# Expert weights in order of use, a new block order, a lighter end of the loop, and first modulation slices on TensorE

## The reference, cut to what matters

```python
c_act = jax.nn.silu(c)                       # one vector of 1024
mod = c_act @ w_ada[l] + b_ada[l]            # 1024 x 6144
sh1, sc1, g1, sh2, sc2, g2 = jnp.split(mod, N_ADA, axis=-1)
u = modulate(rmsnorm(h, norm_mix_g[l]), sh1, sc1)
...
# mixture of experts: 64 experts, each token goes to 8
def expert_block(args):
    toks, ws, e = args
    xb = u_pad[toks]
    hid = jax.nn.silu(xb @ we_gate[e]) * (xb @ we_up[e])
    return (hid @ we_down[e]) * ws[:, None]
```

## Time and profile before

| | |
|---|---|
| median of 3 runs | 3078.28 us (3076.34 to 3078.71) |
| profiled execution | 3077.83 us, span 3076.5 us |
| TensorE matmuls busy | 2711.3 us, 88% |
| VectorE, ScalarE, GpSimd busy | 1058.0, 706.2, 164.7 us |
| DMA | 423.89 MB, mean 138 GB/s over the span |

### The profile page before, as it was taken

How to read it: one execution, slowest core, us unless ns; L and a number is a source line. 1 busy time by engine, 2 the same in 40 slices (tenths; PEclk the granted TensorE clock), 3 DMA queues, 4 the chain that set the end, 5 groups by cost and what they waited for, 6 DMA issues and landing times.

```text
span 3076.5 us, 41132 instructions
## 1 busy us (share of the span) xinstructions
PE 2711.3 (88%) x16972; PEld 1598.5 (52%) x16972; DVE 1058.0 (34%) x2309; ACT 706.2 (23%) x1152; POOL 164.7 (5%) x126
## 2 busy tenths in 40 slices
PE   6999997999989898887989489979996988999797
PEld 2666664444437556564655234437875433555443
DVE  7665654322212212111211231026774113433312
ACT  2333331100011111111111110135552222333311
POOL 0000000000000112222222100000000000000000
PEclk8999998999998899898989789979997999999899
DMA  6222211333313998998898513221101211111110
GB/s 238 104 89 81 70 65 45 123 137 123 133 62 127 350 324 307 346 333 304 299 373 287 180 65 119 66 106 41 64 28 66 83 69 37 55 55 55 35 41 28
DMA packets 80746, 423.89 MB, mean 138 GB/s; under 512 B 16144, under 2 KB 16528, under 8 KB 37936
## 3 DMA queue, kind: packets, MB, share of 16 engines
q1 hardware_dynamic: 53296, 366.37, 30.9%
q0 software_dynamic: 17568, 35.71, 4.9%
q10 hardware_dynamic: 9696, 19.17, 1.7%
HBM read 392.79 MB, written 56.69 MB: 146 GB/s over the span
## 4 chain that ended last, share of the span: by engine, by line
PE 73%; DMA 11%; DVE 8%; ACT 5%; issue 3%; SPq 1%; POOLq 0%; POOL 0%; ACTq 0%; DVEq 0%
PE psum_all L277 33%; PE psum_all L1859 7%; PE psum_all L1419 7%; DMA total_rows<-big,rows 5%; PE psum_all L3253 4%; PE psum_all L2006 4%; PE psum_all L1466 3%; PE psum_all L3126 3%; PE psum_all L287 3%; DMA weights<-t_experts 2%; DMA big<-t_experts 2%; PE psum_all L302 1%; DMA big<-u_rows,rows 1%; PE psum_all L632 1%; DVE big L3387 1%
## 5 line engine op out<-in xcount | busy, mean ns | idle before, releaser
L277 PE MATMUL psum_all<-u,weights 128*128 128x512 f32 x1024 | 451.3, 598 | 12.2 <-issue 12.2
L277 PE MATMUL psum_all<-big,weights 128*128 128x512 f32 (+1 forms) x768 | 338.4, 596 | 6.7 <-DVE big L3419 4.2
L277 PEld LDWEIGHTS psum_all<-u,weights 128*128 128x128 f32 x1024 | 194.3, 192 | 248.0 <-issue 247.6
L1419 PE MATMUL psum_all<-weights,big 128*64 128x256 f32 (+2 forms) x1216 | 249.4, 407 | 49.0 <-DMA weights<-t_experts 35.1
L1419 PE MATMUL psum_all<-big 128*32 128x256 f32 (+2 forms) x1728 | 216.3, 404 | 35.6 <-DMA weights<-t_experts 19.0
L277 PEld LDWEIGHTS psum_all<-big,weights 128*128 128x128 f32 (+1 forms) x768 | 144.7, 189 | 194.6 <-issue 188.0
L1859 PE MATMUL psum_all<-big,weights 128*128 128x512 f32 x512 | 222.4, 597 | 14.0 <-DVE big L1929 14.0
L1419 PEld LDWEIGHTS psum_all<-weights,big 128*64 128x64 f32 (+2 forms) x1216 | 169.5, 160 | 88.3 <-issue 55.4
L1419 PEld LDWEIGHTS psum_all<-big 128*32 128x32 f32 (+2 forms) x1728 | 140.4, 135 | 74.7 <-issue 43.3
L1859 PEld LDWEIGHTS psum_all<-big,weights 128*128 128x128 f32 x512 | 98.1, 192 | 138.2 <-issue 134.8
L287 PE MATMUL psum_all<-const_cols,big 128*128 128x128 f32 (+2 forms) x892 | 129.5, 286 | 38.2 <-DMA big<-u_rows,rows 22.6
(11 more groups left out here) (343 smaller groups left out, 3399.2 us busy)
## 6 DMA issues: line engine op xcount, KB each, us to landing
big<-t_experts SPq DMA_DIRECT2D x96, 1024.0 KB
weights<-t_experts SPq DMA_DIRECT2D x96, 1024.0 KB
weights<-t_ada SPq DMA_DIRECT2D x24, 1024.0 KB, 6.9
weights<-t_rkvg SPq DMA_DIRECT2D x16, 1024.0 KB, 5.4
rwkv_inputs<-big ACTq DMA_DIRECT2D x48, 256.0 KB, 2.0
big<-rwkv_inputs SPq DMA_DIRECT2D x8, 1280.0 KB, 6.6
weights<-t_x SPq DMA_DIRECT2D x8, 1024.0 KB, 4.8
weights<-t_BC SPq DMA_DIRECT2D x8, 1024.0 KB, 4.8
```

The lines of the kernel that those rows point to most:

```text
L277: last = pe.matmul(out, lhsT, rhs, start=n == 0, stop=n == len(terms) - 1)
L1419: ins = pe.matmul(K.psum[rows, bank, n * F_E:(n + 1) * F_E], xT[:, k, rows], X.part(r, n, KD, F_E)[:, k, :], start=k == 0, stop=k == KD - 1)
```

## The change

Four edits:

1. The experts' parts are loaded in the order in which the products use them: for block b the gate parts, then the up parts, then the down parts of block b - 1. The register that holds the expert's number is read anew for each part, behind the wait.
2. `blocks()` yields the same blocks in another order.
3. Behind the loop for overflow blocks only VectorE drains, and only SyncE waits for it, before it loads `total_rows`.
4. For the first eight modulation slices, TensorE does the products: the column of c_act, repeated 32 times, is the stationary operand, the slice (256 columns) is the moving one. Row tile k goes to column group k mod 4, two tiles are accumulated in each group. VectorE copies the 128 x 256 result out, times 1/32, and TensorE sums over the partitions as before. The `pe_sum` products are spread between the slices. The table of constants comes in two loads: its first 256 columns (identity and ones) behind the first part of x, the rest behind all of x.

```diff
@@ start_act
-            act.dma_start(K.consts[:, :], A["shape_consts"][:, 0:CONST_SMALL]).then_inc(*K.consts_in.tick("all_in"))
+            act.dma_start(K.consts[:, 0:FIRST_CONSTS], A["shape_consts"][:, 0:FIRST_CONSTS]).then_inc(*K.ones_in.tick("all_in"))
+    act.dma_start(K.consts[:, FIRST_CONSTS:CONST_SMALL], A["shape_consts"][:, FIRST_CONSTS:CONST_SMALL]) \
+        .then_inc(*K.consts_in.tick("all_in"))
@@
+def pe_ada_rows(K, q, s, i):
+    pe, w, b = K.nc.tensor, K.W.tile(i, KD, 256), 4 + s % 2
+    K.bank(b, q.dve, "rows", s)
+    pe.wait_ge(*K.W.here(i))
+    for k in range(KD):
+        at = 32 * (k % 4)
+        ins = pe.matmul(K.psum[at:at + 32, b, 0:256], K.c_act[:, k:k + 1].to_broadcast([P, 32]), w[:, k, :],
+                        start=k < 4, stop=k >= 4)
+    ins.then_inc(*K.W.left(i, q.pe))
+
+def dve_ada_rows(K, q, s, i):
+    dve = K.nc.vector
+    if s >= 2:
+        dve.wait_ge(*q.pe.at("ada", s - 2))
+    dve.wait_ge(*q.pe.at("w", i))
+    dve.tensor_scalar(K.ada[s % 2][:, :], K.psum[:, 4 + s % 2, 0:256], 1.0 / 32, None, ALU.mult).then_inc(*q.dve.tick("rows", s))
+
+def pe_ada_sum(K, q, s):
+    pe, acc = K.nc.tensor, K.ada[s % 2]
+    pe.wait_ge(*q.dve.at("rows", s))
+    for half in range(2):
+        ins = pe.matmul(K.psum[:, 6, 2 * s + half:2 * s + half + 1], acc[:, half * P:half * P + P], K.c("ones")[:, 0:1],
+                        start=True, stop=True)
+    ins.then_inc(*q.pe.tick("ada", s))
@@ start_pe
+    pe.wait_ge(*q.act.at("c"))
+    for s in range(2):
+        pe_ada_rows(K, q, s, w0 + s)
+    pe.wait_ge(*K.ones_in.at("all_in"))
+    K.bank(6, q.dve, "mod")
+    for s in range(2, 8):
+        pe_ada_sum(K, q, s - 2)
+        if s in (2, 4, 5, 6):
+            k = max(0, 2 * s - 6)
+            pe_sum(K, q, "mix", k)
+            pe_sum(K, q, "mix", k + 1)
+        pe_ada_rows(K, q, s, w0 + s)
+    for s in (6, 7):
+        pe_ada_sum(K, q, s)
     pe.wait_ge(*K.consts_in.at("all_in"))
-    K.bank(6, q.dve, "mod")
-    for s in range(2):
-        pe_ada(K, q, s, w0 + s, 2 * s)
-    for k in range(KD):
-        pe_sum(K, q, "mix", k)
-    for s in range(2, 8):
-        pe_ada(K, q, s, w0 + s, 2 * s)
@@ blocks
-        yield from (alone(8 + 4 * j), alone(9 + 4 * j), two(36 + 5 * j, 37 + 5 * j), alone(10 + 4 * j))
-        yield from (most(24 + 2 * j, 56 + 2 * j), two(38 + 5 * j, 39 + 5 * j), most(25 + 2 * j, 57 + 2 * j))
+        yield from (alone(8 + 4 * j), most(24 + 2 * j, 56 + 2 * j), two(36 + 5 * j, 37 + 5 * j), most(25 + 2 * j, 57 + 2 * j))
         yield from (alone(2 * j), alone(2 * j + 1), more(2 * j, 2 * j + 1, 32 + j))
+        yield from (alone(9 + 4 * j), two(38 + 5 * j, 39 + 5 * j))
         if j % 2:
             yield two(35 + 5 * j, 40 + 5 * j)
-        yield alone(11 + 4 * j)
+        yield from (alone(10 + 4 * j), alone(11 + 4 * j))
@@
-ORDER = list(dict.fromkeys(r for parts in BLOCKS for r, _, _, _ in parts))
-LOAD_OF = {r: 3 * x for x, r in enumerate(ORDER)}
+def parts_in_order():
+    for b in range(NB + 1):
+        if b < NB:
+            for n in range(2):
+                yield from ((r, n) for r, _, _, _ in BLOCKS[b])
+        if b > 0:
+            yield from ((r, 2) for r, _, _, _ in BLOCKS[b - 1])
+
+ORDER = list(dict.fromkeys(parts_in_order()))
+LOAD_OF = {part: i for i, part in enumerate(ORDER)}
@@ moe_sp
-    for x, r in enumerate(ORDER):
+    for i, (r, n) in enumerate(ORDER):
+        if i >= X.RING:
+            sp.wait_ge(*part_left(q, i - X.RING))
+        elif i >= 6:
+            sp.wait_ge(*K.W.gone(next(j for j in range(w0 + 4, w0 + 10) if j % K.W.N == i - 6)))
         e = sp.value_load(K.number[0:1, 2 + r:3 + r], min_val=0, max_val=E_ALL - 1)
-        for n in range(3):
-            i = 3 * x + n
...
@@ extra_blocks
-    for lane in lanes:
-        lane.drain().then_inc(K.turns_over, 1)
-    for lane in lanes:
-        lane.wait_ge(K.turns_over, len(lanes))
+    nc.vector.drain().then_inc(*K.turns_over.tick("all over"))
@@ join_sp
     K.nc.sync.wait_ge(*K.added.at(NB - 1))
+    K.nc.sync.wait_ge(*K.turns_over.at("all over"))
```

More of the change, by code:

```diff
@@ L105, in const_table @@
     put("ones", np.ones((P, P)))
+    first = sum(x.shape[1] for x in parts)
     put("upper", r <= c)
@@ L146, in const_table @@
     put("sin", sin)
-    return np.concatenate(parts, axis=1), cols, small
-CONSTS, CONST_COLS, CONST_SMALL = const_table()
+    return np.concatenate(parts, axis=1), cols, first, small
+CONSTS, CONST_COLS, FIRST_CONSTS, CONST_SMALL = const_table()
 VECTORS = (("conv_w", 128), ("conv_b", 32), ("ssd_norm_g", 16), ("b_ada", 48), ("c", 8), ("norm_mix_g", 8),
@@ L386, in start_dve @@
         dve.memset(K.eps[:, n:n + 1], eps).then_inc(*q.dve.tick(*(("eps",) if n == 3 else ())))
-    dve.wait_ge(*q.act.at("c"))
     for s in range(8):
-        dve_ada(K, q, s, w0 + s, q.pe.at("ada", s - 2) if s >= 2 else None)
+        dve_ada_rows(K, q, s, w0 + s)
     K.nc.vector.wait_ge(*q.act.at("mix", "rstd"))
@@ L1068, in part @@
     def part(self, r, n, rows, cols):
-        return self.ring[(LOAD_OF[r] + n) % self.RING][:, 0:rows * cols].rearrange("p (k n) -> p k n", n=cols)
+        return self.ring[LOAD_OF[r, n] % self.RING][:, 0:rows * cols].rearrange("p (k n) -> p k n", n=cols)
 def part_here(K, r, n):
-    i = LOAD_OF[r] + n
+    i = LOAD_OF[r, n]
     return K.expert_in[i % Moe.RING].at(i)
 def part_left(q, i):
-    r, n = ORDER[i // 3], i % 3
+    r, n = ORDER[i]
     return q.pe.at(("gate", "gate up", "down")[n], LAST_USE[r])
@@ L1093, in moe_sp @@
     sp.wait_ge(*q.dve.at("order"))
-    for x, r in enumerate(ORDER):
-        e = sp.value_load(K.number[0:1, 2 + r:3 + r], min_val=0, max_val=E_ALL - 1)
-        for n in range(3):
-            i = 3 * x + n
[L1098 to L1103, removed]
+    for i, (r, n) in enumerate(ORDER):
[3 more added lines that the diff above has]
+            sp.wait_ge(*K.W.gone(next(j for j in range(w0 + 4, w0 + 10) if j % K.W.N == i - 6)))
+        e = sp.value_load(K.number[0:1, 2 + r:3 + r], min_val=0, max_val=E_ALL - 1)
+        sp.dma_start(X.ring[i % X.RING], A["t_experts"][ds(e * P, P), n * 2048:(n + 1) * 2048]) \
+            .then_inc(*K.expert_in[i % X.RING].tick(i))
 def rows_pe(K, X, q):
@@ L3603, in build_program @@
     K = Kernel(nc, book)
-    K.vec_in, K.consts_in, K.cs_out, K.cs_in = (K.new_signal(n) for n in ("vec_in", "consts_in", "cs_out", "cs_in"))
+    K.vec_in, K.ones_in, K.consts_in, K.cs_out, K.cs_in = (K.new_signal(n) for n in ("vec_in", "ones_in", "consts_in", "cs_out", "cs_in"))
     K.x_in = [K.new_signal(f"x_in{n}") for n in range(4)]
@@ L3615, in build_program @@
     K.turn_weights = [K.new_turns(f"turn_weights{n}") for n in range(3)]
-    K.turns_over, K.waits_alone = nc.alloc_semaphore("turns_over"), nc.alloc_semaphore("waits_alone")
+    K.turns_over, K.waits_alone = K.new_signal("turns_over", 1), nc.alloc_semaphore("waits_alone")
     K.expert_in = [K.new_signal(f"expert_in{n}") for n in range(Moe.RING)]
```

## The result

The changed kernel takes 3043.69 us (median of 4 runs, 3040.51 to 3045.14) against 3077.31 us for the kernel before on the same chip: ratio 0.9894, 95% interval 0.9876 to 0.9911. The forecast was 3045 us. The profiled execution took 3044.45 us, its span 3043.1 us is 33.4 us shorter than before. One execution of the kernel with the start alone took 5935.6 us; it is a slow run and left out of that kernel's median and ratio.

What follows compares the result with a forecast made beforehand. The prediction took the serial chain of adds to be nearly the expert stage's bound, with VectorE's chain late at the start. Start -12.5, stage -20 and loop end -0.5 gave -33, so 3045 us from 3078.28; range 3005 to 3068.

Steps and rivals of the forecast that it cites:

- Start, -11.3 at the modulation: Kernel start: slices on TensorE bring the first modulation to 34 us instead of 45.27; bounds 2 and 12.2.
- `decay_pe`, -1.2: Start, behind the modulation: shorter TensorE idle time ahead means fewer slow-clock passes, 1.2 us less; bounds 0 and 2.0.
- Expert stage, -20: Expert stage: 30 us of slack gone, 12 back in longer adds, 2 less at the end; bounds +4 and -63.
- rival A: Expert stage: adds hardly bind, DMA work limits the gain; stage -67, kernel 2998 us; chance 0.07.
- slack 30: Expert stage: GpSimd's serial add chain has 30 us of idle time to lose, taking 6.1 us per unwaited add.
- adds longer 12: Expert stage: DMA share rises from 0.90 to 0.935, making the 72 adds 12 us longer in all.
- The 2 us for the two one-add blocks at the end: End of expert stage: two one-add blocks come last instead of one, worth about 2 us.
- One mark of the prediction: Expert stage, sign of being right: GpSimd waits for the add before in more than 60 of 71 cases.
- mark for the pitch, 8.4 to 8.8 us: Expert stage, sign of being right: a mean add pitch of 8.4 to 8.8 us, gathers' time subtracted.
- rival C: Expert stage: adds spaced as beside loads, pitch 9.4 us, stage 39 us longer, kernel 3104 us; chance 0.07.
- the rule alone: Expert stage: DMA queues served in turn by packets, so steadier loads slow adds and give back nearly all the slack.
- Loop end, -0.5: End of the overflow loop: dropping the five-engine meeting saves 0.5 us; bounds 0 and -1.4.

Runs made afterwards that it cites:

- the start alone: Kernel before with only the first eight modulation slices moved to TensorE, constants in two loads and norm sums between slices: 3067.9 us, ratio 0.9974.
- late constants: Changed kernel with the rest of the constants (0.75 MB) loaded only behind the norm's rstd on ScalarE: 3046.06 us, ratio 0.9892 against the kernel before.

## Why the prediction was right, step by step

**Start, -11.3 at the modulation: 10.3 measured.** The mechanism and each price held: 1.07 and 1.93 us for a slice's products (0.9 and 1.8 predicted), a copy of 0.42 us (0.4). The way from slice 7's arrival to the modulation took 2.4 us, where the prediction's lower bound had 2.1. What was off is the arrival of slice 7: about 32.6 us, not 31.0. The small load behind it, issued at 19.05 us, took 13.8 us to land where it had taken 12.0. That the bytes in front are the same held; that they arrive in the same time did not. The run with late constants shows that 0.75 MB fewer in front bring the modulation 1.4 us forward; why the same bytes took 1.6 us longer (the first 128 KB of constants now come in rows of 1 KB, for one) was not tried.

**`decay_pe`, -1.2: +0.4 measured.** This step failed, and just missed its bound of 0. It took it that TensorE's idle time ahead would be shorter, but TensorE waited 2.44 us for u right before `decay_pe` in both traces. Before, the clock was at 0.50 when `decay_pe` began at 47.60 us and came back at 52 us; after, it fell to 0.50 at 35.7 us, and was back at 42.5 us, when `decay_pe` had run since 37.32 us. So some 5.2 us of it ran at 1.2 GHz, against 4.4 us before.

```profile
46.00:48.00 2.00, 0.40 (x1) 0.18 (x2) 2.00 (x4) 1.26 (x2) 0.00 (x0) 0.50 0.93 393
...
50.00:52.00 2.00, 2.00 (x4) 0.51 (x3) 1.57 (x5) 2.00 (x4) 0.00 (x0) 0.51 0.00 0
```

**Expert stage, -20: 18.8 measured** up to the issue of the last add. The reading that the waits TensorE names are not what the stage can gain was right, and rival A, which went by them (-67), is out: 81 us of weight waits went and 56 came back as waits for gathered rows. The term "slack 30" was right by the adds' semaphore: 30.5 us were there and 27.5 of them went. That the prediction picked it out of 6 to 73 us by taking 6.1 us for adds that no row showed is luck in part. The term "adds longer 12" came out as 8, but not by its reasoning: it had the DMA share rise from 0.90 to 0.935, and the share was 0.91 (1024 to 1670 us); the 8 us lie within the spread of the mean add, so no run shows this term. The 2 us for the two one-add blocks at the end can't be told from spread; the block order alone gave -0.6 us, interval -4.6 to +3.4. One mark of the prediction was off: waits for the add before came 57 times, not over 60. Its mark for the pitch, 8.4 to 8.8 us, holds by its own formula, (683 - 64 - 3) / 72 = 8.6 us. But the gathers' 64 us, which that formula subtracts, mostly lie under an add that is in flight (1131.93 to 1132.99 us under the add of 1130.09), so the pitch at which adds follow each other is about 683 / 72 = 9.5 us, and was 9.75. The slack doesn't depend on this; the pitches given for rival C do.

**Adds beside loads.** The Trainium skill ("DMA: Bandwidth & Descriptors", Queues, rings and completion order) says each engine takes its queues in turn by packets. The slower adds beside loads agree with that (10.28 against 5.82 us above), but the mean add grew by only 0.11 us between the two profiles. So at most 8 of the 27.5 us were given back, and not nearly all of them, as it would be by the rule alone.

**Loop end, -0.5: 0.7 to 0.9** by the distance from the last add to the load. The prediction had the five-engine meeting cost something behind the add's landing, and it did.

**Sum.** The terms erred by 1.0, 1.6, 1.2 and about 0.3 us. As measured they come to 10.3 - 0.4 + 18.8 + 0.7 = 29.4 us, against 33 forecast; the other 4 us of the 33.4 come from code that is the same, 2.9 of them behind the expert stage, where the spread is larger than that. So that the forecast was within 2 us of the median is luck in part. Of the 7 us by which unchanged stages differ, the mean add accounts for some (7.02 us in the shortest of the four with the old order of loads, 7.14 us in the longest); why adds differ from one execution to the next was not looked into.

## What to carry to other kernels

The largest wait of the busiest engine tells what that engine runs into next, not what its removal brings: here 81 us of waits went and the stage gained 19.6 us. Follow the slower chain beside it from end to end, count its idle time, and take that as the gain. Where two near-equal bounds lie side by side, try their remedies together before dropping either: here 20 and 18 us one at a time, 90 together in the stage. A chain of accumulating DMAs in which each waits for the landing before it can bind by these waits while the DMA engines still have room; dealing the adds to a second target tensor shows which of the two it is, and here took 71 us off the stage.

## What the runs showed of the hardware

Adds in DRAM by indirect DMA overlap well: with up to two in flight each took longer (9.84 against 7.14 us from the end of its issue to its last rise), but the DMA share was 0.95, where the changed kernel's stretches beside loads had 0.87 to 0.93, and 72 adds that had taken 683 us fitted into 611 (1025.1 to 1635.9 us) with TensorE as the bound. Float32 products with 32 stationary columns in four column groups run side by side: 16 passes of 256 columns in 1.07 us at 2.4 GHz, 0.067 us each, against 7.15 / 32 = 0.22 us for full-width passes, 3.3 times the pace.
